# Preparing the delta-rule recurrence between the input projection's tiles, in one stage instead of two

## The reference

```python
h = rms_norm(x, norm_in_g[l])
p = h @ w_in[l]                       # 1024 -> 2176 (recurrence) + others
# rwkv7_group, on the first 2176 columns
pf = pf + mu * (prev - pf)            # prev: the row of the token before
r, k, v, gate, wd, ad = split_cols(pf, RWKV_SIZES)     # 4 x 512, 64, 64
w_log = -jax.nn.softplus(-(w0 + jnp.tanh(wd) @ w_up)) - 0.5
decay = jnp.exp(-jnp.exp(w_log))
a = jax.nn.sigmoid(a0 + ad @ a_up)
kk = k * k_k
k = k * (1.0 + (a - 1.0) * k_a)
kk = kk / jnp.maximum(jnp.sqrt(jnp.sum(kk * kk, axis=-1, keepdims=True)), 1e-12)  # per head of 64
y = rwkv7_scan(r, decay, k, v, kk, a)
...
y = y + jnp.sum(r * k * r_k, axis=-1, keepdims=True) * v
```

## Time and profile before

| | before |
|---|---|
| median of 3 runs | 2032.19 us (2029.75 to 2034.1) |
| profiled execution: time | 2032.1 us |
| its span, first to last instruction | 2030.0 us |
| PE busy | 1864.8 us (92%) |
| DVE, ACT, POOL busy | 918.1, 838.2, 252.3 us |
| mean granted TensorE clock | 0.954 of full |

### The profile page before, as it was taken

The page is one execution under the profiler, slowest core; times in us unless marked ns, Lnnn a source line. Parts: engine busy times, 40 slices in busy tenths (PEclk is TensorE's granted clock), DMA queues, the critical chain, the costliest instruction groups (busy, mean ns, idle before and its releaser), DMA issues. The chain is left out here.

```text
span 2030.0 us, 31550 instructions
## 1 busy us (share of the span) xinstructions
PE 1864.8 (92%) x12644; PEld 1462.6 (72%) x12644; DVE 918.1 (45%) x1600; ACT 838.2 (41%) x1372; POOL 252.3 (12%) x209
## 2 busy tenths in 40 slices
PE   6993999979889889989999999999999899999997
PEld 5871566467577557667888888878887778888885
DVE  2438344363436668544333333364554443333333
ACT  4342444335434244534344432285563344434222
POOL 3002232200012400002000000042221120000000
PEclk9995999969989989999999999999998999999998
DMA  5220001300022100011232332222220213333331
GB/s 177 86 85 0 25 31 34 113 6 2 1 83 68 43 1 1 2 60 60 95 97 93 99 98 94 78 94 72 74 66 31 83 54 94 101 94 94 102 94 52
DMA packets 38340, 133.82 MB, mean 66 GB/s; under 512 B 4880, under 2 KB 5200, under 8 KB 37968
## 3 DMA queue, kind: packets, MB, share of 16 engines
q1 hardware_dynamic: 37360, 130.00, 20.3%
q10 hardware_dynamic: 864, 2.17, 0.3%
HBM read 129.27 MB, written 2.10 MB: 65 GB/s over the span
## 5 line engine op out<-in xcount | busy, mean ns | idle before, releaser
L138 DVE TENSOR_TENSOR big_parts<-ring,big_parts 128x1024 fp32r<-128x1024 f32 x164 | 204.8, 1250 | 527.0 <-ACT big_parts L133 527.0
L164 PE MATMUL bank<-h_parts,big_parts 128*128 128x512 f32 x960 | 381.5, 397 | 10.3 <-DVE big_parts L138 6.5
L165 PE MATMUL bank<-y_parts,big_parts 128*128 128x512 f32 x960 | 375.7, 391 | 0.0
L166 PE MATMUL bank<-h_parts,big_parts 128*128 128x512 f32 x960 | 375.7, 391 | 0.0
L133 ACT ACTIVATE big_parts<-ring 128x1024 fp32r<-128x1024 f32 x164 | 173.7, 1061 | 285.6 <-PE bank L166 285.3
L164 PEld LDWEIGHTS bank<-h_parts,big_parts 128*128 128x128 f32 x960 | 181.1, 189 | 57.2 <-issue 12.6
L166 PEld LDWEIGHTS bank<-h_parts,big_parts 128*128 128x128 f32 x960 | 181.4, 189 | 38.5
L165 PEld LDWEIGHTS bank<-y_parts,big_parts 128*128 128x128 f32 x960 | 181.6, 189 | 35.9
L165 PE MATMUL bank<-y_parts,work_parts 128*128 128x512 f32 x368 | 145.9, 397 | 0.0
L172 PE MATMUL bank<-cst 128*128 128x256 f32 x464 | 136.9, 415 | 4.3 <-PEq L90 4.3
L164 PE MATMUL bank<-big_parts 128*128 128x512 f32 x352 | 136.9, 389 | 0.0
(11 more groups left out here) (386 smaller groups left out, 2957.1 us busy)
## 6 DMA issues: line engine op xcount, KB each, us to landing
ring<-in_wstream SPq DMA_DIRECT2D x229, 512.0 KB, 3.6
x<-in_xt SPq DMA_DIRECT2D x8, 512.0 KB, 7.5
out_t<-x SPq DMA_DIRECT2D x8, 256.0 KB, 2.0
work<-in_memt ACTq DMA_DIRECT2D x1, 1024.0 KB, 14.8
work<-in_cw SPq DMA_DIRECT2D x1, 1024.0 KB, 5.8
cst<-in_cst ACTq DMA_DIRECT2D x1, 704.0 KB, 7.9
cos<-in_reset SPq DMA_DIRECT2D x2, 256.0 KB, 2.6
big<-work SPq DMA_DIRECT2D x4, 128.0 KB, 4.4
```

The costliest lines, as they stand in the source:

```text
L138: dve.tensor_tensor(self.parts[:, self.place_of(n), 1, :, :], self.ring[:, n % RING, :, :], self.parts[:, self.place_of(n), 0, :, :].bitca ...
L164: pe.matmul(out, w[0], x[0], start=start, stop=False, skip_group_check=True)
L165: pe.matmul(out, w[0], x[1], start=False, stop=False, skip_group_check=True)
L166: return pe.matmul(out, w[1], x[0], start=False, stop=stop, skip_group_check=True)
```

## The change

Stage 2 is gone; what it did stands between the tiles of stage 1. The stream's order is now: four k tiles, `wa`, four r tiles (these nine are the "head"), the memory's four slabs, then v and gate. Work that needs k and `wa` alone begins after tile 5. On PE the memory's sums of squares stand directly behind the first two tiles, the gate logits behind the last tile. The squares of the keys of all heads are summed into one bank: each m fills 32 of its partitions (16 equal rows per head), so that one square root, one maximum and one reciprocal serve all four m; a small selection matrix `pick` spreads the result back to 128 partitions (`key_spread`). Buffers move: the keys' norms, exclusive and inclusive sums live in tiles 17 to 28 of `c.big`, the rounded parts of h in `c.hr` instead of `work`. The 256 KB table `reset` is loaded ahead of the first slab, and the constants grow by one matrix of 64 KB. Some 300 more PE instructions are written out, since a loop of 12 tiles is unrolled.

In the diff below come first the new PE parts and PE's order, then ACT's order up to the memory's keys, DVE's from tile 9 on, and SP's. On ACT `tile_out(i)` waits for tile i's matmuls, casts the slab two ahead and copies the bank; `gates(m)` is the two sigmoids, each of which frees an up bank (`up_out`). On DVE `shift(i)` is the split of the slab two ahead and the shifted add; `products_a` holds the operations of the old lines 577, 578, 580 and 581, `products_b` those of 582, 583, 584 and 586, `bonus_out` that of 590. Behind tile 16 DVE adds the gate's bias and makes the last `bonus_out`.

```diff
+RW_ORDER = (*range(PR_K, PR_K + 4), PR_WA, *range(PR_R, PR_R + 4), *range(PR_V, PR_V + 4), *range(PR_G, PR_G + 4))
+RW_HEAD = 9
...
+            def key_sums():
+                for m in range(4):
+                    pe.wait_ge(sq_out, m + 1)
+                    mm = pe.matmul(sums_bank[32 * m:32 * m + 32, :], con(c, "blk")[:, 0:P:4], n[:, m, :], start=True, stop=True)
+                mm.then_inc(sums_made, 1)
+            def key_spread(m):
+                pe.wait_ge(inv_out, 1)
+                if m >= 2:
+                    pe.wait_ge(n_out, m - 1)
+                at = slice(32 * m, 32 * m + 32)
+                pe.matmul(spread_banks[m % 2][:, :], con(c, "pick")[at, :], inv[at, :], start=True, stop=True,
+                          tile_position=(32 * m, 0)).then_inc(spread, 1)
+            def ups(m):
+                pe.wait_ge(tanh, 1)
+                for j in range(2):
+                    if m:
+                        pe.wait_ge(up_out, 2 * (m - 1) + j + 1)
+                    at = HALVES[j]
+                    pe.matmul(up_banks[j][:, :], c.wup[at, m * P:(m + 1) * P], wa[at, 0, :], start=True, stop=True).then_inc(up_made, 1)
+            def bonus(m):
+                pe.wait_ge(rk_out, m + 1)
+                if m >= 2:
+                    pe.wait_ge(y_out, m - 1)
+                pe.matmul(rk_banks[m % 2][:, :], con(c, "blk"), iclr[:, m, :], start=True, stop=True).then_inc(rk_made, 1)
...
             warm(c, pe, c.bank[4], 6)
+            first_pair(c, pe, 0, hp)
+            for t in range(KT):
+                pe.wait_ge(squares, t + 1)
+                mm = pe.matmul(c.bank[6][:, 0:M], con(c, "ones"), squares_m[:, t, :], start=t == 0, stop=t == KT - 1)
+            mm.then_inc(stats, 1)
+            for i in range(2, 6):
+                tile(i)
+            key_sums()
+            tile(6)
+            pe.wait_ge(roots, 1)
+            ups(0)
+            tile(7)
+            ups(1)
+            key_spread(0)
+            tile(8)
+            ups(2)
+            key_spread(1)
+            mem_keys(0)
+            ups(3)
+            mem_keys(1)
+            key_spread(2)
+            mem_values()
+            key_spread(3)
+            for i in range(RW_HEAD, RW_TILES):
+                tile(i)
+                if i in (11, 13, 15):
+                    bonus((i - 11) // 2)
+            gate_logits()
+            bonus(3)
...
+            for i in range(RW_HEAD):
+                tile_out(i)
...
+                if i == 5:
+                    act.wait_ge(sums_made, 1)
+                    act.activation(inv, sums_bank[:, :], ACT.Sqrt).then_inc(root_out, 1)
+                    act.wait_ge(free[0], 2)
+                    act.activation(wa[0:HD, 0, :], wa[0:HD, 0, :], ACT.Tanh).then_inc(tanh, 1)
+                if i >= 7:
+                    gates(i - 7)
+            for j in range(2):
+                c.slab_done_wait(act, n_mem + j)
+                c.cast_slab(act, n_mem + PARTS + j)
+                act.activation(c.km[:, j, :], c.bank[1 + j][:, 0:M], ACT.Copy).then_inc(mem_out, 1)
+                gates(2 + j)
...
+            for i in range(RW_HEAD, RW_TILES):
+                shift(i)
+                m = (i - RW_HEAD) // 2
+                if (i - RW_HEAD) % 2 == 0:
+                    products_a(m)
+                else:
+                    products_b(m)
+                    if m:
+                        bonus_out(m - 1)
...
+            bonus_out(3)
...
+            sp.dma_start(c.reset[:, :], a["reset"]).then_inc(reset_in, 16)
+            c.load_slabs(sp, 0, PLAN["ns"] + RING)
```

More of the change, by code:

```diff
@@ L342, in _, with tile_out @@
             act.wait_ge(omu_ready, 1)
[L343 to L347, removed]
+            def tile_out(i):
+                t = RW_ORDER[i]
+                c.slab_done_wait(act, slab(i))
+                if slab(i) + PARTS < PLAN["ns"]:
+                    c.cast_slab(act, slab(i) + PARTS)
+                act.activation(c.big[:, t, :], c.bank[i % RING][:, :], ACT.Copy, scale=c.omu[:, t:t + 1]).then_inc(scaled, 1)
@@ L394, in _ @@
-            mm.then_inc(stats, 1)
[L395 to L433, removed]
+            def tile(i):
+                c.slab_wait(pe, slab(i))
+                if RW_HEAD <= i < RW_HEAD + 4:
+                    pe.wait_ge(mem_out, i - RW_HEAD + 1)
+                elif i >= RING:
+                    pe.wait_ge(free[i % RING], i // RING)
+                for t in range(KT):
+                    mm = product(pe, c.bank[i % RING][:, :], c.slab_parts(slab(i), t), hp.tile(t), t == 0, t == KT - 1)
+                mm.then_inc(c.slab_done, 1)
@@ new lines, in mem_keys, with mem_values @@
+            def mem_keys(j):
+                c.slab_wait(pe, n_mem + j)
+                pe.wait_ge(free[1 + j], 2)
+                for t in range(KT):
+                    mem.wait(pe, t)
+                    mm = product(pe, c.bank[1 + j][:, 0:M], c.slab_parts(n_mem + j, t), mem.tile(t), t == 0, t == KT - 1)
+                mm.then_inc(c.slab_done, 1)
+            def mem_values():
+                for j in range(2):
+                    c.slab_wait(pe, n_mem + 2 + j)
+                pe.wait_ge(free[3], 2)
+                pe.wait_ge(free[0], 3)
+                for j in range(2):
+                    for t in range(KT):
+                        at = c.place_of(n_mem + 2 + t // 4)
+                        w = [c.parts[:, at, p, 2 * (t % 4):2 * (t % 4) + 2, :].rearrange("p a b -> p (a b)") for p in range(2)]
+                        mm = product(pe, c.bank[(3 + j) % RING][:, 0:M], [x[:, j * P:(j + 1) * P] for x in mem.tile(t)], w,
+                                     t == 0, t == KT - 1)
+                        if j == 1 and t % 4 == 3:
+                            mm.then_inc(c.slab_done, 1)
+                    if j == 0:
+                        mm.then_inc(mem_done, 1)
@@ new lines, in gate_logits @@
+            def gate_logits():
+                pe.wait_ge(n_out, 3)
+                for q in range(QT):
+                    for t in range(KT):
+                        for half in HALVES:
+                            mm = pe.matmul(c.bank[4][half, 12 * q:12 * q + 12], c.x[:, t, q * P:(q + 1) * P][:, half], c.wgl[:, t, :],
+                                           start=t == 0, stop=t == KT - 1)
+                mm.then_inc(gl_done, 1)
+            warm(c, pe, c.bank[4], 6)
+            first_pair(c, pe, 0, hp)
@@ L447, in _ @@
                                          ALU.mult, ALU.mult).then_inc(h_ready, 1)
[L449 to L454, removed]
+            dve.wait_ge(reset_in, 16)
@@ L455, in _ @@
+            for i in range(RW_HEAD):
+                shift(i)
+                if i == 2:
                     dve.wait_ge(roots, 1)
@@ L629, in stage_rwkv_chunks @@
     u, ysb, st = (wk(c, 14336 + T * i, T) for i in range(3))
-    yt = wk(c, 8192, 4, T)
+    yt = c.y[:, 0:4, :]
     pcb = c.pcb
```

292 lines of the change are left out of this document (140 added, 152 removed).

## The result

The changed kernel takes 2003.83 us (median; 2003.11 to 2010.8 in four of its five runs), the kernel before 2032.19 us. The ratio is 0.9875, with a 95% interval of 0.9847 to 0.9902. The fifth run of the first series was disturbed (mean granted clock 0.756), and it was the profiled one, so the rows here come from the profiled run of the same kernel in the second series: 2010.83 us, span 2009.0 us.

What follows compares the result with a forecast made beforehand. PE bounds the input tiles (106.17 of 108 us busy), DVE the preparation (48.24 of 57.80). PE's walk, 164.6, plus 3.4 for clock starts the recurrence at 168.0, not 199.17: 2032.1 - 31.1 = 2001.0 us, range 1994 to 2012 (8 in 10).

Steps and rivals of the forecast that it cites:

- The direction and the price of hiding: Input tiles and preparation: each preparation step hides under a tile's 5.44 us; uncovered, 48.24 us of DVE would come back.
- The walk along PE: Sum of PE's steps from 26.0 us to the recurrence's first matmul: 164.6 us, before clock drops.
- key sums: Four sums on PE between tiles 5 and 6: 1.3 us, from 61.9 to 63.2, bounds 0.8 and 3.3.
- waits for sigmoids: PE waits for ACT to free the up banks before the second, third and fourth pair: 3.8, 2.5, 2.3 us.
- slip beside POOL: Tiles 9 to 16: DVE's products slow down beside POOL and delay a head sum once, +1.0 us.
- The tail: From tile 16 to the recurrence: gate logits, last head sum at half clock, DVE and stage border, 7.5 us.
- the wait for slab 13: After the last spread, before tile 9, PE waits for this slab's split: 0.4 us.
- Changes between full and partial arrays: Between tiles and partial-array matmuls on PE: not in the sum; a rival took some 14 at 0.2, 2.8 us.
- the clock term: PE's clock halves after two of its waits or the tail, 1.7 us each: +3.4 us, giving 168.0.
- a start after 178 us: Sign of being wrong: the recurrence's first matmul comes after 178 us, where 168 was forecast.
- the wait of 1.8 us before 38.96: Kernel before, PE waiting for slab 2: 1.81 us that left the clock at 1.00, cited for the clock estimate.
- the first rival: PE before the recurrence: all four waits drop the clock (3.4 us more), array changes cost 2.8; 2007 us, 15%.

Runs made afterwards that it cites:

- products_last: Changed kernel with DVE's products of all four m and the head sums put behind tile 16 instead of between tiles 9 to 16: 2025.86 us.
- pool_late: Changed kernel with POOL's four products made to wait for tile 13: 2010.94 us in one run.
- gates_early: Changed kernel with each pair of sigmoids made one tile earlier on ACT: 1989.08 us, 0.9797 of the kernel before.
- warm_waits: Changed kernel with PE's three waits for sigmoids filled by 7, 5 and 4 matmuls into unread banks: 2000.8 us, 0.9843 of the kernel before.
- after_again: The changed kernel run once more, unchanged, for a profile at the usual clock: 2009.62 us.
- four_recips: Changed kernel with the shared maximum and reciprocal split into four of 32 partitions each: 2003.2 us, 0.9882 of the kernel before.
- stats_late: Changed kernel with the memory's sums of squares behind tile 3 again, ACT's root two tiles and DVE's reciprocal one tile later: 2011.91 us.
- short_tail: gates_early with the gate logits behind tile 11 and all of m = 3's products in round 15: 1988.8 us, 0.9779 of the kernel before.

## Why the prediction was right, and where it was not

**The direction and the price of hiding**: right. PE bounded the tiles, DVE the preparation, and nearly all of the preparation hides; products_last shows it for the products, 18.3 us of DVE's work, by taking them back (+13.3 us at the recurrence's start, +16.2 in the median).

**The walk along PE**, against the changed kernel's rows: key sums begin at 62.8 (61.9 forecast; PE's start was 0.5 us later), and with tile 6 they take 6.73 us to 69.54, so 1.29 for the sums (1.3 forecast). The waits for sigmoids, 3.89, 2.47, 2.17 (3.8, 2.5, 2.3). From the last spread to the gate logits 123.37 to 172.02, 48.65 us (108.9 to 157.1, 48.2), with 0.75 us of slip beside POOL (1.0). The tail 6.76 us (7.5; its last head sum ran at full clock here, 1.13, and at half in pool_late). Loading `reset` first and the wait for slab 13 cost nothing to speak of.

**Changes between full and partial arrays** weren't in the sum, and they do have a price. The matmul rows overlap, so a missing gap shows nothing; the starts do. Here are the tile's matmuls around an up pair, around a pair with a spread, and around a head sum, which uses the full array, in gates_early at full clock:

```profile
68.94 0.39 PE L168 MATMUL bank<-h_parts,work_parts 128*128 128x512 f32 x1
70.65 0.39 PE L167 MATMUL bank<-y_parts,work_parts 128*128 128x512 f32 x1
75.68 0.39 PE L168 MATMUL bank<-h_parts,work_parts 128*128 128x512 f32 x1
78.44 0.40 PE L167 MATMUL bank<-y_parts,work_parts 128*128 128x512 f32 x1
131.80 0.39 PE L168 MATMUL bank<-h_parts,work_parts 128*128 128x512 f32 x1
133.17 0.39 PE L167 MATMUL bank<-y_parts,work_parts 128*128 128x512 f32 x1
```

From a tile's last matmul to the next tile's second it is 1.71 us with a pair between, 2.76 with a pair and a spread, 1.37 with a head sum. Two steps of 0.23 us belong to the tiles; that leaves 1.25, 2.30 and 0.91. So a pair costs 0.34 more than a head sum, 0.17 for each of its two changes, and pair and spread 0.48 more than two head sums, 0.16 for each of three. What in the change takes the time, these rows don't say. In the forecast a pair or a spread was 0.82, so some dozen changes outside the waits, an estimate of 2 us, were missing; of the key sums' 1.29 us, 0.3 are such changes too.

**The step that failed is the clock term**, "I take two drops: +3.4". It was 11.5 us by warm_waits. The prediction had named a start after 178 us as a sign of being wrong, and 178.78 is one. I let the wait of 1.8 us before 38.96, after which the clock had stayed, stand for the two shorter waits, and took 3.4 us at half clock for each drop. In the run all four waits ahead of 119 us have a stretch at 0.50 in or behind them, 10.2, 6.8, 6.8 and 3.4 us long: 27.3 us in place of 6.8, and half of the part in which PE worked is some 12 to 13 us. So number and length were both too small. That is the first rival's mechanism, in both halves: all four waits end in a drop (in this profile; not so in warm_waits and gates_early), at 1.7 times its 6.8 us, and the changes of the array have a price, 0.16 to 0.17 where it had 0.2. The rival gave 2007 us and a chance of 15%. Sum with 11.5 in place of 3.4: 164.6 + 11.5 = 176.1, and 0.9 for the later key sums makes 177.0 of the 178.8; the changes of the array are of the size of the rest.

**Why 2001.0 was still near 2003.83.** The start came 10.8 us late, the median 2.8. The difference lies behind the stage, and isn't shown to be the change's doing: the same 11,904 matmul records take 1830.2 us in after_again and 1823.1 in four_recips, whose code there is the same. The two rows are the whole later part of each, by the columns of the earlier trace rows:

```profile
178.78:2009.00 1830.22, 1722.97 (x11904) 1353.06 (x11904) 818.65 (x1477) 763.53 (x1259) 222.53 (x179) 0.96 0.19 63
```

```profile
177.83:2000.90 1823.07, 1715.73 (x11904) 1347.53 (x11904) 818.90 (x1477) 763.41 (x1259) 222.62 (x179) 0.97 0.20 64
```

DVE, ACT and POOL are equal to 0.3 us; PE is 7.2 us longer at a mean clock lower by 0.01: it is at half clock for 139 us of this part in the first and 122 us in the second. The other profiles stand on either side: 1829.4 to 1832.6 us in six more kernels, the one before among them, and 1823.6 in stats_late. So in later stages the clock falls in one run and not in another. The changed kernel, four_recips and stats_late have two groups of times some 7 to 8 us apart; in the kernel before, 6 of its 22 runs on the first chip and in the first series are at 2024.7 to 2026.9 and the others from 2029.75 on, a narrower gap, and gates_early and products_last show no clear groups. The first series caught the changed kernel mostly in its lower group, the kernel before mostly in its upper one. Group against group, by medians, the change is worth 22 to 23 us (2025.8 to 2003.4, 2033.1 to 2010.0), near its stage's 20.4. So the total came near by luck, not by the walk; what decides in which group a run falls is open.

## What to carry to other kernels

Work of an idle engine is hidden well between the tiles of a busy one, but a handshake of two engines placed inside this row (here two banks, freed behind the next tile's cast) makes short waits on TensorE, and each can cost as much again in clock: here 10.0 us in four waits and 11.5 us of clock. Order the helper engine's work so that it frees the bank one tile ahead (gates_early, 20.5 us for a few lines of ACT's order, and with short_tail the best kernel here at 1989); where that can't be, matmuls into a dead bank keep the clock. And compare a stage by its own start and end in the profile when whole-program times come in groups.

## What the runs showed of the hardware

- Four float32 matmuls with 32 output columns each, on separate column groups, take 1.10 us together; one of 128 columns takes 1.03 to 1.13. They run at once.
- A change between full and partial arrays takes 0.16 to 0.17 us of TensorE's time (gates_early), though no idle time is shown.
- A DVE reciprocal of 512 elements takes 3.34 us over 32 partitions and 3.35 over 128.
- Beside a POOL product, DVE's products of 0.69 us took 1.66 us (pool_late, 156.92 and 158.62), its split the usual 1.24 us (154.21), and then POOL's product took 2.3 us in place of 1.3.
- Waits of 2.2 to 3.9 us on TensorE, between tile 7 and the memory's values, were each followed by half clock in all profiles that have them, for 3.4 to 10.2 us. After waits of 1.5 to 1.9 us it went either way: the clock fell after 1.48 us in after_again (at 116 us) and after 1.58 us in short_tail, and stayed at full after 1.48 us in warm_waits and stats_late, 1.58 us in gates_early, 1.88 us in stats_late (at 39.5 us) and, in the kernel before, even 2.63 us.
